# Masks through TensorE, three levels written in place, and two exponentials moved to the end of the in-projection, in a fused two-block kernel

## The chip, the cores and the metric

One core of a Trainium2 chip runs the whole program. The metric is device time in microseconds (us); the kernel before takes 3434.22 us, the median of three runs. Engine names are those of the profile: PE is TensorE (PEld its weight loads), DVE is VectorE, ACT is ScalarE, POOL is GpSimd, SP is SyncE, whose queue issues the loads of weights.

## What is computed

Two transformer-like blocks on 256 tokens of width 1024 run one after the other, each of two layers. The change lies in the first block, in the mixers of its two layers. Cut to what matters there:

```python
mod = cond @ w_ada[l] + b_ada[l]          # modulation, needed by later layers and sublayers
qa, fa, ia, ga, qb, kb, vb, ... = split((x * (1 + sc1) + sh1) @ w_in[l])
# mixer A, 4 heads of 128: a gated linear recurrence, as scores with decay
log_f = log(lb + (1 - lb) * sigmoid(fa));  k = (1 - lb) * sigmoid(-fa);  b = cumsum(log_f)
o_t = sum_{s <= t} (q_t . (k_s * exp(b_t - b_s))) v_s
oa = head_rms_norm(o) * silu(ga)
# mixer B, 8 heads of 64: stick-breaking attention, s < t only
z = q k^T / 8
w_ts = exp(log_sigmoid(z_ts) + sum_{s<j<t} log_sigmoid(-z_tj));   ob = w v
```

All values are float32.

## The kernel before

The 256 tokens are two tiles (TT) of 128. Each layer first runs `input_projection` (L1102): seven products of hT with 512 columns of `w_in`. A product's weights come in four quarters; ScalarE copies each quarter in rounded form (`split_hi`, L337) when TensorE has used up the quarter that held the place, and VectorE makes the remainder (L350). While the seventh product runs, ScalarE makes the rounded quarters of the tile that follows. VectorE takes the logarithms of the gates through `tensor_tensor_scan` (L1181), eight running sums over 128 tokens each, into B; that is done at the fifth product. The program is cut into blocks by hand (`nc.Block`), and every block begins and ends with a barrier of all five engines: the block of the in-projection ends at L3925, the mixer block begins at L1318.

The mixer block (`mixers`, L1302) runs both mixers at once, and its order is written out by hand for each engine.

*The recurrence.* For pairs of tokens s < t within 128, exp(b_t - b_s) is made in seven levels of halves, of 64, 32, 16, 8, 4, 2 and 1 tokens: with b at the end of a first half as the middle, exp(b_t - mid) goes to the queries of the second half and exp(mid - b_s) to the keys of the first. For each level n, VectorE subtracts (L1435, L1437), ScalarE takes one exponential over 128x1024 (L1401), VectorE multiplies into `qe` and `ke` (L1449, L1450), TensorE forms eight 128x128 products (4 heads by 2 tiles, L1353) in one of two PSUM units, and VectorE merges the right elements into `scores` with `copy_predicated` and a mask of that level (`take`, L1422). The diagonal (s = t) comes first (L1345). After the levels the cross-tile part, queries of tile 1 against keys of tile 0, takes the same way: L1458 and L1459, L1401, L1465 and L1466, L1363. At the end TensorE multiplies `scores` by the values (L1373, L1376), and VectorE copies the outputs (L1475). Each level's product also waits until `ke` and `qe` may be overwritten.

*Stick-breaking.* Four groups g of two heads (`StickBreaking`) are laid between the levels, one for two levels. `scores` (PE, L1229) forms the three causal 128x128 blocks of each head; `sizes` (ACT, L1259, L1260) copies them to Y and takes the absolute value L; `logs` (ACT, L1264, L1265) makes log(1 + exp(-L)), which needs another activation table than the exponential; `losses` (DVE, L1275) adds max(Y, 0) and then multiplies the two diagonal blocks by the 0/1 mask `before` (L1278); `sums` (PE, L1237 to L1239) forms suffix sums; `rest` (DVE, L1283) subtracts them and adds -1e30 on the masked elements of the diagonal blocks (L1285); `weights` (ACT, L1269) takes the exponential, `values` (PE, L1250, L1252) multiplies, `keep` (DVE, L1290, L1291) stores.

*The fills.* Between these steps TensorE forms the products of the modulation vectors of later sublayers (`beside`, L901): 24 halves of a tile in layer 0 and 20 in layer 1, 1 MB of weights each, how many where is written in `BESIDE_VALUES` and `BESIDE_LEVELS`. Four halves fit in the buffer `raw`: SP issues the load of a half when the fourth half before it has been used.

The orders of TensorE and ScalarE in that block are these loops (`n` counts levels, g = n // 2):

```python
for n in range(NL):                 # TensorE; odd n: stick.sums(g)
    stick_step(n)                   # even n: stick.scores(g), stick.values(g - 1), fill
    pe.wait_ge(vec_ready.sem, vec_ready.at(1 + n))
    ...                             # the level's products
    fill(BESIDE_LEVELS[l][n])
for n in range(NL + 1):             # ScalarE
    if n and n % 2 == 0:
        stick.sizes(act, s_, n // 2)
    act.wait_ge(cols_ready.sem, cols_ready.at(1 + n))
    act.activation(E[:], E[:], ACT.Exp).then_inc(act_ready.sem, 1)
    ...                             # n = 0: sizes(0); even n: logs, odd n: weights
```

## Time and profile before

| | before |
|---|---|
| median of 3 runs (lowest, highest) | 3434.22 us (3434.17, 3435.14) |
| span of the profiled execution, first to last instruction | 3432.0 us |
| TensorE / VectorE / ScalarE / GpSimd busy | 85% / 69% / 31% / 28% |
| mean granted clock of TensorE | 0.930 of full speed |
| mixer block, layer 0: first product to VectorE's copy of the outputs | 65.75 us |
| mixer block, layer 1: first instruction of VectorE to its copy of the outputs | 60.17 us |

The record of the profiled execution gives its span; the time of a run is taken around the program and is 2.2 us above that span at the median. A busy TensorE is not TensorE at its peak, and its two granted levels of clock in this trace are 0.50 (1.2 GHz) and 1.00 (2.4 GHz); a stretch in which it changes shows a value between. In the trace a float32 matmul appears as two rows, so eight products are "x16". In a timeline row the bracket says how long the engine was idle before the instruction and what released it.

### The profile page before, as it was taken

The page shows a single profiled execution, that of the slowest core. Times are in us where ns is not written, and L with a number is a line of the kernel's source. Part 1 is how long each engine was busy: PE and PEld are TensorE (multiplying, and loading weights), DVE is VectorE, ACT ScalarE, POOL GpSimd, SP SyncE. Part 2 cuts the span into 40 slices and gives each one's busy share as a digit, 9 for nine tenths or more (in the row PEclk, how much of TensorE's full clock was granted, in tenths as well). Part 3 has the DMA queues.
Part 4 walks back from the last instruction along what each step waited for, and adds up shares of the span by engine and source line. Part 5 has one row for each costly group of instructions (what it writes and reads, how often), then busy time and mean ns, then how long its engine had stood idle before and what let it go on. Part 6 is the DMA issues. An engine that isn't in the chain of part 4 may idle for free. (4 is left out here: it accounts for less than half of the span.)

```text
span 3432.0 us, 39790 instructions
## 1 busy us (share of the span) xinstructions
PE 2914.4 (85%) x14720; PEld 2169.4 (63%) x14720; DVE 2371.9 (69%) x3824; ACT 1048.4 (31%) x1586; POOL 971.8 (28%) x1028
## 2 busy tenths in 40 slices
PE   8899679948599879898699525777999999999999
PEld 6687368437387328685386212222788888887887
DVE  4657966677877766758876886565665765757665
ACT  3544110011100114543200101111444554546653
POOL 0000054555644670000354667777100000000000
PEclk9999689969799999998699758999999999999999
DMA  8765999999999996657999999999555455553253
GB/s 319 265 215 199 422 392 422 415 409 417 382 404 413 402 405 218 255 181 290 406 405 415 418 401 406 420 401 398 190 187 168 160 189 178 181 174 126 87 192 127
DMA packets 224262, 1034.12 MB, mean 301 GB/s; under 512 B 28784, under 2 KB 31344, under 8 KB 166256
## 3 DMA queue, kind: packets, MB, share of 16 engines
q0 software_dynamic: 147456, 536.94, 39.0%
q1 hardware_dynamic: 76656, 495.19, 39.0%
q8 instruction: 93, 1.52, 0.2%
q14 instruction: 57, 0.47, 0.0%
HBM read 1030.98 MB, written 1.05 MB: 301 GB/s over the span
## 5 line engine op out<-in xcount | busy, mean ns | idle before, releaser
L350 DVE TENSOR_TENSOR w_lo<-raw,w_hi 128x1024 fp32r<-128x1024 f32 (+1 forms) x460 | 546.9, 1204 | 415.1 <-ACT w_hi L337 414.0
L2238 POOL DMA_INDIRECT arena_layer<-in_peer_u,arena_layer x512 | 483.3, 944 | 1169.1 <-DVE arena_layer L2148 716.0
L2304 DVE CUSTOM_DVE_ANT_0 arena_layer<-arena_layer,ps 128x1024 f32<-128x1024 f32 x512 | 605.1, 1218 | 154.5 <-DMA arena_layer<-in_peer_u,arena_layer 124.9
L337 ACT ACTIVATE w_hi<-raw 128x1024 fp32r<-128x1024 f32 (+1 forms) x460 | 478.1, 1043 | 577.2 <-PE ps L745 371.1
L2300 DVE SCALAR_TENSOR_TENSOR ps<-arena_layer,ps 128x1024 f32<-128x1024 f32 x336 | 432.9, 1289 | 237.6 <-DMA arena_layer<-in_peer_v,arena_layer 225.7
L2238 POOL DMA_INDIRECT arena_layer<-in_peer_v,arena_layer x512 | 488.3, 954 | 272.7 <-DVE ps L2300 157.0
L801 PE MATMUL ps<-hT,w_hi 128*128 128x512 f32 x1376 | 479.7, 394 | 1.5 <-DVE hT L2956 1.5
L2338 PE MATMUL ps<-arena_layer,parts_context 128*128 128x512 f32 x704 | 351.1, 626 | 111.5 <-DMA arena_layer<-in_peer_v,arena_layer 104.5
L804 PE MATMUL ps<-hT,w_lo 128*128 128x256 f32 x1376 | 384.5, 279 | 0.0
L2338 PEld LDWEIGHTS ps<-arena_layer,parts_context 128*128 128x128 f32 x704 | 124.1, 194 | 335.7 <-issue 292.1
L745 PE MATMUL ps<-parts_context,w_whole 128*128 128x256 f32 x1216 | 271.3, 386 | 44.7 <-PEq L1044 44.7
L745 PE MATMUL ps<-hT,w_hi 128*128 128x256 f32 x1664 | 301.1, 284 | 4.1 <-DVE hT L1772 1.8
L801 PEld LDWEIGHTS ps<-hT,w_hi 128*128 128x128 f32 x1376 | 257.8, 187 | 61.6 <-issue 2.6
L745 PE MATMUL ps<-parts_context,raw 128*128 128x256 f32 x1280 | 280.6, 381 | 12.0 <-PEq L1044 12.0
L745 PEld LDWEIGHTS ps<-parts_context,w_whole 128*128 128x128 f32 x1216 | 235.6, 194 | 79.1 <-issue 45.9
L745 PEld LDWEIGHTS ps<-parts_context,raw 128*128 128x128 f32 x1280 | 244.8, 191 | 46.2 <-issue 12.4
L745 PEld LDWEIGHTS ps<-hT,w_hi 128*128 128x128 f32 x1664 | 259.4, 192 | 6.1 <-issue 6.0
L804 PEld LDWEIGHTS ps<-hT,w_lo 128*128 128x128 f32 x1376 | 259.6, 189 | 0.0
L745 PE MATMUL ps<-hT,w_lo 128*128 128x256 f32 x832 | 235.4, 283 | 0.0
L745 PE MATMUL ps<-w_hi,parts_ffn_x 128*128 128x512 f32 x704 | 220.7, 395 | 0.0
L745 PE MATMUL ps<-w_hi,hT 128*128 128x512 f32 x512 | 161.4, 397 | 4.1 <-DVE hT L1011 3.3
L745 PEld LDWEIGHTS ps<-hT,w_lo 128*128 128x128 f32 x832 | 159.6, 192 | 0.0
(405 smaller groups left out, 3500.2 us busy)
## 6 DMA issues: line engine op xcount, KB each, us to landing
raw<-in_ffn_w_gu SPq DMA_DIRECT2D x122, 1024.0 KB
raw<-in_ffn_w_down SPq DMA_DIRECT2D x54, 1024.0 KB
raw<-in_w_ada SPq DMA_DIRECT2D x44, 1024.0 KB
raw<-in_w_in SPq DMA_DIRECT2D x44, 1024.0 KB
raw<-in_w_mod SPq DMA_DIRECT2D x40, 1024.0 KB
w_whole<-in_w_mod SPq DMA_DIRECT2D x32, 1024.0 KB
w_whole<-in_ffn_w_gu SPq DMA_DIRECT2D x32, 1024.0 KB
raw<-in_conv_w_in SPq DMA_DIRECT2D x18, 1024.0 KB
```

The costliest lines, as they stand in the source:

```text
L337: act.activation(self.hi[:, k, 0:g.chunks(t)[k] * g.cols], self.part(g, t, slot, k // 2, g.starts(t, k), g.starts(t, k + 1)), ACT.Copy).th ...
L350: dve.tensor_tensor(self.lo[:, k, 0:n], self.part(g, t, slot, k // 2, g.starts(t, k), g.starts(t, k + 1)), self.hi[:, k, 0:n].bitcast(F32) ...
L745: mm = pe.matmul(out_, stay, move, start=start and n == 0, stop=stop and n == len(combos) - 1, skip_group_check=True)
L801: pe.matmul(both.rearrange("p (k t) -> p k t", k=2), high[:, c, cols], hT_both[:, :, row, :], start=row == 0, stop=False, skip_group_check ...
L804: mm = pe.matmul(both[:, 0:SEQ], low[:, c, cols], hT_hi[:, row, :], start=False, stop=row == last, skip_group_check=True)
L2238: gp.indirect_dma_start(self.grow[:, slot % GR, :], None, self.tables[slot // half_way], bass.IndirectOffsetOnAxis(ap=self.index[:, k:k + ...
L2300: dve.scalar_tensor_tensor(out=self.tile, in0=row, scalar=cell, in1=self.tile, op0=ALU.mult, op1=ALU.add) \
L2304: dve.tensor_tensor_reduce(row, row, self.tile, 1.0, 0.0, ALU.mult, ALU.add, cell).then_inc(row_used.sem, 1)
L2338: mm = pe.matmul(ps[:, t, cols], self.diagonals[:, side, r, :], self.grow[:, k % GR, cols], start=opens and r == 0, stop=True, skip_group_ ...
```

## The change

It does three things in the mixers of both layers.

1. *Masks of stick-breaking.* `scores` accumulates four more products, identity by `before_neg` (-1e30 on the masked elements, 0 elsewhere), onto the diagonal blocks of the scores in PSUM. The masking instructions of `losses` and `rest` on VectorE go, and with them the constant `before` and its load.
2. *Levels in place.* For the first three levels (DIRECT = 3: 64, 32, 16) TensorE forms only the small products that count, m by m, and writes each to its place in one PSUM unit: 8, 16 and 32 products instead of 8 each. One `take` with a merged mask reads all three, at the level of 8.
3. *Edge exponentials.* The exponentials of the first level and of the cross-tile part leave the mixer block. ScalarE makes them at the end of `input_projection`, from B directly: the subtraction becomes a bias operand, one instruction for each of 8 blocks and half (16 of 128x64), one of 128x4x128 and four of 128x128, into two new buffers in `side`. VectorE's subtractions for these two go, as does ScalarE's 128x1024 exponential for each.

In the rows below, `side_layer` holds the new buffers (first_E, cross_E), `rows` holds B, E and `qe`, `arena_layer` `ke` and `scores`, `w_hi` the rounded quarters, `columns` the identity.

ScalarE, end of layer 0's in-projection and start of the mixer block, before:

```order
L337 ACTIVATE w_hi<-raw 128x1024 [waits quarters_used,half_landed_3]
L337 ACTIVATE w_hi<-raw 128x1024 [waits quarters_used]
L3925 UNCONDITIONAL_BRANCH
L1393 UNCONDITIONAL_BRANCH [waits barrier_Pool_Activation_PE_DVE_SP_release]
L1401 ACT_TABLE_LOAD
L1401 ACTIVATE rows<-rows 128x1024 [waits cols_ready]
L1259 ACTIVATE arena_layer<-ps 128x768 [waits stick_scores_made]
L1260 ACTIVATE y_tok<-ps 128x768
```

and with the change:

```order
L338 ACTIVATE w_hi<-raw 128x1024 [waits quarters_used,half_landed_3]
L338 ACTIVATE w_hi<-raw 128x1024 [waits quarters_used]
L1215 ACTIVATE stat<-rows 128x8 [waits log_gates_summed]
L1218 ACT_TABLE_LOAD
L1218 ACTIVATE side_layer<-rows 128x64 x8
L1221 ACTIVATE side_layer<-rows,stat 128x64 [waits middle_sums_negated]
L1221 ACTIVATE side_layer<-rows,stat 128x64 x7
L1223 ACTIVATE side_layer<-rows 128x4x128
L1225 ACTIVATE side_layer<-rows 128x128 x4
L3970 UNCONDITIONAL_BRANCH
L1436 UNCONDITIONAL_BRANCH [waits barrier_Pool_Activation_PE_DVE_SP_release]
L1288 ACTIVATE arena_layer<-ps 128x768 [waits stick_scores_made]
```

The two branch rows are the end of one block and the start of the next, with the barrier between them. The new instructions stand after the last rounded quarter and before the barrier; the first 128x1024 exponential after the barrier is gone.

TensorE, layer 0's mixer block from the first scores to the second, before:

```order
L1229 MATMUL ps<-arena_layer 128x256 x2
L1229 MATMUL ps<-arena_layer 128x128 x2
L901 MATMUL ps<-first_layer_275,side_layer 32x512 [waits first_beside_tile_landed]
L901 MATMUL ps<-first_layer_275,side_layer 32x512 x7
L1353 MATMUL ps<-rows,arena_layer 128x128 [waits vec_ready]
L1353 MATMUL ps<-rows,arena_layer 128x128 x7
L901 MATMUL ps<-raw,side_layer 32x512 [waits half_landed_0]
```

and with the change:

```order
L1254 MATMUL ps<-arena_layer 128x128 x2
L1258 MATMUL ps<-before_neg,columns 128x128 x4
L904 MATMUL ps<-first_layer_274,side_layer 32x512 [waits first_beside_tile_landed]
L904 MATMUL ps<-first_layer_274,side_layer 32x512 x7
L1384 MATMUL ps<-rows,arena_layer 64x64 [waits vec_ready]
L1384 MATMUL ps<-rows,arena_layer 64x64 x7
L904 MATMUL ps<-raw,side_layer 32x512 [waits half_landed_0]
```

The four mask products stand between the scores and the first fill; the level of 64 has 64x64 products.

VectorE, layer 0, from the first `losses` to the first `keep`, before:

```order
L1275 SCALAR_TENSOR_TENSOR y_tok<-arena_layer,y_tok 128x768 [waits stick_logs_made]
L1278 TENSOR_TENSOR y_tok<-y_tok,before 128x2x2x128 [waits vec_step]
L1422 COPY_PREDICATED arena_layer<-level_mask,ps 128x1024 [waits pe_done]
L1449 TENSOR_TENSOR rows<-arena_layer,rows 128x16x32 [waits pe_done,act_ready,vec_step]
L1450 TENSOR_TENSOR arena_layer<-arena_layer,rows 128x16x32 [waits vec_step]
L1283 TENSOR_TENSOR y_tok<-arena_layer,ps 128x768 [waits stick_losses_summed,vec_ready]
L1285 TENSOR_TENSOR y_tok<-y_tok,before_neg 128x2x2x128 [waits vec_step]
L1435 TENSOR_TENSOR rows<-rows 128x32x16
L1437 TENSOR_TENSOR rows<-rows 128x32x16 [waits vec_step]
L1422 COPY_PREDICATED arena_layer<-level_mask,ps 128x1024 [waits pe_done]
L1290 CAST parts_layer<-ps 128x256 [waits stick_values_summed,vec_step]
L1291 TENSOR_TENSOR parts_layer<-ps,parts_layer 128x256 [waits vec_step]
```

and with the change:

```order
L1304 SCALAR_TENSOR_TENSOR y_tok<-arena_layer,y_tok 128x768 [waits stick_logs_made]
L1466 COPY_PREDICATED arena_layer<-level_mask,ps 128x1024 [waits pe_done]
L1496 TENSOR_TENSOR rows<-arena_layer,rows 128x16x32 [waits pe_done,act_ready,vec_step]
L1497 TENSOR_TENSOR arena_layer<-arena_layer,rows 128x16x32 [waits vec_step]
L1309 TENSOR_TENSOR y_tok<-arena_layer,ps 128x768 [waits stick_losses_summed,vec_ready]
L1480 TENSOR_TENSOR rows<-rows 128x32x16
L1482 TENSOR_TENSOR rows<-rows 128x32x16 [waits vec_step]
L1314 CAST parts_layer<-ps 128x256 [waits stick_values_summed]
L1315 TENSOR_TENSOR parts_layer<-ps,parts_layer 128x256 [waits vec_step]
```

Two masking instructions and one predicated copy are gone from this piece; the waits are the same.

The diff, cut to its core:

```diff
 LEVELS = (64, 32, 16, 8, 4, 2, 1)
+DIRECT = 3
...
+            edge_exponentials(act, B, *edges)
...
-                            dve.tensor_tensor_scan(
+                            ins = dve.tensor_tensor_scan(
                                 B[:, b * P:(b + 1) * P], ones[:], sg[:, h, m * P:(m + 1) * P], 0.0,
                                 ALU.mult, ALU.add)
+                    ins.then_inc(gates_summed.sem, 1)
...
+    def edge_exponentials(act, B, E, Ec):
+
+
+        m = LEVELS[0]
+        blocks = HG_HEADS * TT
+        b3, e3 = [ap.rearrange("p (b t) -> p b t", t=P) for ap in (B, E)]
+        b4, c4 = [ap.rearrange("p (h t m) -> p h t m", t=TT, m=P) for ap in (B, Ec)]
+        turned_middles = stat[:, 24:24 + blocks]
+        act.wait_ge(gates_summed.sem, gates_summed.at(1))
+        act.activation(turned_middles, b3[:, :, m - 1], ACT.Copy, scale=-1.0) \
+           .then_inc(middles_turned.sem, 1)
+        for b in range(blocks):
+            act.activation(e3[:, b, 0:m], b3[:, b, 0:m], ACT.Exp, bias=b3[:, b, m - 1:m], scale=-1.0)
+        act.wait_ge(middles_turned.sem, middles_turned.at(1))
+        for b in range(blocks):
+            ins = act.activation(e3[:, b, m:P], b3[:, b, m:P], ACT.Exp, bias=turned_middles[:, b:b + 1])
+        ins.then_inc(edge_expd.sem, 1)
+        act.activation(c4[:, :, 1, :], b4[:, :, 1, :], ACT.Exp)
+        for h in range(HG_HEADS):
+            ins = act.activation(c4[:, h, 0, :], b4[:, h, 0, :], ACT.Exp,
+                                 bias=b4[:, h, 0, P - 1:P], scale=-1.0)
+        ins.then_inc(edge_expd.sem, 1)
...
-                    mm = pe.matmul(self.bank[n][:, cols], self.kb[at, g, keys], self.qb[at, g, queries],
-                                   start=True, stop=True)
+                    pe.matmul(self.bank[n][:, cols], self.kb[at, g, keys], self.qb[at, g, queries],
+                              start=cols.start == 0, stop=False, skip_group_check=True)
+            for n in range(2):
+                for cols in (slice(0, P), slice(SEQ, self.WIDTH)):
+                    mm = pe.matmul(self.bank[n][:, cols], ident[:], before_neg[:],
+                                   start=False, stop=True, skip_group_check=True)
             mm.then_inc(sb_scored.sem, 1)
...
-            v.link(dve.scalar_tensor_tensor(out=L, in0=self.Y, scalar=0.0, in1=L,
-                                            op0=ALU.max, op1=ALU.add))
-            mask = before[:].unsqueeze(1).unsqueeze(1).to_broadcast([P, 2, 2, P])
-            dve.tensor_tensor(self.edges(L), self.edges(L), mask, ALU.mult).then_inc(sb_lost.sem, 1)
+            dve.scalar_tensor_tensor(out=L, in0=self.Y, scalar=0.0, in1=L,
+                                     op0=ALU.max, op1=ALU.add).then_inc(sb_lost.sem, 1)
 
         def rest(self, dve, v, g):
-            S = self.S
             dve.wait_ge(sb_summed.sem, sb_summed.at(g + 1))
-            v.link(dve.tensor_tensor(S, self.Y, self.banks, ALU.subtract))
-            neg = before_neg[:].unsqueeze(1).unsqueeze(1).to_broadcast([P, 2, 2, P])
-            dve.tensor_tensor(self.edges(S), self.edges(S), neg, ALU.add).then_inc(sb_left.sem, 1)
+            dve.tensor_tensor(self.S, self.Y, self.banks, ALU.subtract).then_inc(sb_left.sem, 1)
...
+                def level_in_place(m):
+
+
+                    for b in range(blocks):
+                        for first in range(0, P, 2 * m):
+                            keys = slice(b * P + first, b * P + first + m)
+                            queries = slice(b * P + first + m, b * P + first + 2 * m)
+                            mm = pe.matmul(ps[first:first + m, 0, queries], ke[:, keys], qe[:, queries],
+                                           start=True, stop=True, skip_group_check=True)
+                    return mm
...
                     pe.wait_ge(vec_ready.sem, vec_ready.at(1 + n))
-                    for b in range(blocks):
-                        mm = pe.matmul(ps[:, (n + 1) % 2, b * P:(b + 1) * P],
-                                       ke[:, b * P:(b + 1) * P], qe[:, b * P:(b + 1) * P],
-                                       start=True, stop=True)
+                    if n < DIRECT:
+                        mm = level_in_place(LEVELS[n])
+                    else:
+                        for b in range(blocks):
+                            mm = pe.matmul(ps[:, unit_of(n + 1), b * P:(b + 1) * P],
+                                           ke[:, b * P:(b + 1) * P], qe[:, b * P:(b + 1) * P],
+                                           start=True, stop=True)
...
-                    if n and n % 2 == 0:
+                    if n % 2 == 0:
                         stick.sizes(act, s_, n // 2)
-                    act.wait_ge(cols_ready.sem, cols_ready.at(1 + n))
-                    act.activation(E[:], E[:], ACT.Exp).then_inc(act_ready.sem, 1)
-                    if n == 0:
-                        stick.sizes(act, s_, 0)
+                    if 0 < n < NL:
+                        act.wait_ge(cols_ready.sem, cols_ready.at(n))
+                        act.activation(E[:], E[:], ACT.Exp).then_inc(act_ready.sem, 1)
...
                 def take(n):
 
+                    if 1 <= n < DIRECT:
+                        return
                     dve.wait_ge(pe_done.sem, pe_done.at(n + 1))
-                    mask = level_mask[:, n, :].unsqueeze(1).to_broadcast([P, blocks, P])
+                    mask = level_mask[:, n and n + 1 - DIRECT, :].unsqueeze(1).to_broadcast([P, blocks, P])
                     v.link(dve.copy_predicated(
                         scores.rearrange("p (b t) -> p b t", t=P), mask,
-                        ps[:, n % 2, :].rearrange("p (b t) -> p b t", t=P)))
+                        ps[:, unit_of(n), :].rearrange("p (b t) -> p b t", t=P)))
...
+                    e_lo, e_hi = halves(E if n else first_E)
+                    if n:
+                        b_lo, b_hi = halves(B)
+                        mid = b_lo[:, :, m - 1:m].to_broadcast([P, nb, m])
+                        v.tick(dve.tensor_tensor(e_hi, b_hi, mid, ALU.subtract))
+                        v.wait()
+                        dve.tensor_tensor(e_lo, mid, b_lo, ALU.subtract).then_inc(cols_ready.sem, 1)
...
-                    dve.wait_ge(act_ready.sem, act_ready.at(1 + n))
                     if n >= 1:
+                        dve.wait_ge(act_ready.sem, act_ready.at(n))
                         dve.wait_ge(pe_done.sem, pe_done.at(n + 1))
+                    else:
+                        dve.wait_ge(edge_expd.sem, edge_expd.at(1))
                     v.link(dve.tensor_tensor(halves(qe)[1], halves(q_all)[1], e_hi, ALU.mult))
...
-                v.link(dve.tensor_copy(te[:, :, 1, :], tb[:, :, 1, :]))
-                dve.tensor_tensor(te[:, :, 0, :], tb[:, :, 0, P - 1:P].to_broadcast([P, HG_HEADS, P]),
-                                  tb[:, :, 0, :], ALU.subtract).then_inc(cols_ready.sem, 1)
+                tiles = [ap.rearrange("p (h t m) -> p h t m", t=TT, m=P) for ap in (cross_E, qe, ke, q_all, k_all)]
+                te, tq, tk, tqa, tka = tiles
                 stick.losses(dve, v, NL // 2)
                 take(NL - 1)
-                dve.wait_ge(act_ready.sem, act_ready.at(1 + NL))
+                dve.wait_ge(edge_expd.sem, edge_expd.at(2))
```

## Rows read from the trace of the kernel before

**Rows 1.** Page, part 1: busy time, share of the span and instructions of each engine.

```profile
PE 2914.4 (85%) x14720; PEld 2169.4 (63%) x14720; DVE 2371.9 (69%) x3824; ACT 1048.4 (31%) x1586; POOL 971.8 (28%) x1028
```

**Rows 2.** Stretches, the two mixer blocks: length, each engine's busy time, PEclk, DMA share, GB/s.

```profile
120.39:186.14 65.75, 59.35 (x458) 36.07 (x460) 47.75 (x64) 36.76 (x38) 0.00 (x0) 0.96 0.90 358
...
1380.87:1441.04 60.17, 54.60 (x426) 35.14 (x428) 47.71 (x63) 36.74 (x38) 0.00 (x0) 0.97 0.86 327
```

**Rows 3.** Timeline of VectorE, layer 1: start, length, engine, line, operation, [idle before <-releaser].

```profile
1379.25 1.22 DVE L1193 COPY arena_layer<-ps 128x1024 f32<-128x1024 f32 x1
...
1380.87 0.69 DVE L1435 TENSOR_TENSOR rows<-rows 128x512 f32<-128x512 f32 x1 [0.40 <-PEq L3925]
...
1389.90 0.96 DVE L1275 SCALAR_TENSOR_TENSOR y_tok<-arena_layer,y_tok 128x768 f32<-128x768 f32 x1 [3.63 <-ACT y_tok L1265]
...
1390.90 0.69 DVE L1278 TENSOR_TENSOR y_tok<-y_tok,before 128x512 f32<-128x512 f32 x1
...
1391.51 1.30 DVE L1422 COPY_PREDICATED arena_layer<-level_mask,ps 128x1024 f32<-128x1024 uint32 x1
...
1392.85 0.69 DVE L1449 TENSOR_TENSOR rows<-arena_layer,rows 128x512 f32<-128x512 f32 x1
...
1400.75 0.69 DVE L1449 TENSOR_TENSOR rows<-arena_layer,rows 128x512 f32<-128x512 f32 x1 [0.72 <-ACT rows L1401]
...
1406.59 0.69 DVE L1449 TENSOR_TENSOR rows<-arena_layer,rows 128x512 f32<-128x512 f32 x1
...
1427.23 0.72 DVE L1449 TENSOR_TENSOR rows<-arena_layer,rows 128x512 f32<-128x512 f32 x1 [0.30 <-ACT rows L1401]
...
1441.04 1.23 DVE L1475 COPY y_tok<-ps 128x1024 f32<-128x1024 f32 x1 [3.04 <-PE ps L1376]
```

**Rows 4.** Timeline of ScalarE, layer 1.

```profile
1377.02 1.06 ACT L337 ACTIVATE w_hi<-raw 128x1024 fp32r<-128x1024 f32 x1 [1.60 <-PE ps L745]
...
1403.63 1.28 ACT L1401 ACT_TABLE_LOAD   x1
...
1404.92 1.06 ACT L1401 ACTIVATE rows<-rows 128x1024 f32<-128x1024 f32 x1
```

**Rows 5.** Timeline of TensorE, layer 0's mixer block.

```profile
120.39 3.75 PE L1345 MATMUL ps<-arena_layer 128*128 128x128 f32 x16 [3.88 <-PEq L3925]
...
162.33 1.06 PE L901 MATMUL ps<-raw,side_layer 128*32 128x512 f32 x8 [0.92 <-DMA raw<-in_w_ada]
...
177.20 1.06 PE L901 MATMUL ps<-raw,side_layer 128*32 128x512 f32 x8 [0.91 <-DMA raw<-in_w_ada]
```

**Rows 6.** Timeline of ScalarE elsewhere: small instructions.

```profile
828.78 7.12 ACT L3391 ACTIVATE rows<-columns 128x128 f32<-128x128 f32 x24 [30.26 <-PEq L3335]
...
190.11 0.21 ACT L1409 ACTIVATE stat<-stat 128x8 f32<-128x8 f32 x1 [5.92 <-DVE stat L1480]
...
190.23 0.57 ACT L1941 COPY side_layer<-ps 128x512 f32<-128x512 f32 x1
```

**Rows 7.** Timeline of TensorE, layer 1.

```profile
1380.86 2.84 PE L1345 MATMUL ps<-arena_layer 128*128 128x128 f32 x16 [3.88 <-PEq L3925]
...
1394.32 2.05 PE L1353 MATMUL ps<-rows,arena_layer 128*128 128x128 f32 x16 [0.65 <-DVE arena_layer L1450]
...
1438.06 1.38 PE L1373 MATMUL ps<-arena_layer 128*128 128x128 f32 x10 [0.51 <-DVE arena_layer L1471]
...
1448.20 1.04 PE L1386 MATMUL ps<-columns,y_tok 128*128 128x128 f32 x8
...
1448.99 0.48 PE L745 MATMUL ps<-hT,w_hi 128*128 128x256 f32 x2
```

**Rows 8.** Stretches of 1 us at the two blocks' starts, columns as before.

```profile
120.00:121.00 1.00, 0.61 (x3) 0.65 (x4) 0.61 (x1) 0.66 (x1) 0.00 (x0) 0.50 0.00 0
...
1381.00:1382.00 1.00, 1.00 (x10) 1.00 (x10) 0.97 (x2) 1.00 (x1) 0.00 (x0) 0.94 0.37 66
```

**Rows 9.** Timeline of TensorE elsewhere: a train of narrow products.

```profile
325.61 3.84 PE L1843 MATMUL ps<-arena_layer 64*128 64x128 f32 x64 [1.10 <-ACT arena_layer L1858]
```

More of the change, by code:

```diff
@@ L3946, in _build @@
             assert beside.tiles == BESIDE_MIXERS[l]
-            input_projection(block, l, qa, sg, km, ia, ga, qb, kb, vb, rows[:, 0, :], (rows[:, 2, :], ke, scores),
-                             beside, arrive)
+            edges = [side[:, 1024 + k * D:1024 + (k + 1) * D] for k in range(2)]
+            input_projection(block, l, qa, sg, km, ia, ga, qb, kb, vb, rows[:, 0, :], edges,
+                             (rows[:, 2, :], ke, scores), beside, arrive)
         oaT, obT = (oa_hi, oa_lo), (ob_hi, ob_lo)
```

48 lines of the change are left out of this document (22 added, 26 removed).

## The prediction

> **What bounds the kernel now.** I read four views in this order: the page for the engines' shares, the timelines of VectorE, ScalarE and TensorE over the two mixer blocks, the table of stretches for TensorE's granted clock, and single rows elsewhere for prices. Over the whole span TensorE is busy 85% and VectorE 69% [rows 1], but the change touches two blocks of 65.75 and 60.17 us, one in each layer [rows 2], so only their own rows count.
>
> In layer 1, the mixer block begins when VectorE has evacuated the last product of the in-projection: that copy ends at 1379.25 + 1.22 = 1380.47 and VectorE's first instruction starts at 1380.87 [rows 3]. ScalarE has finished its last split copy at 1377.02 + 1.06 = 1378.08 [rows 4] and waits for the block's barrier. Inside the block, which I take up to VectorE's copy of the outputs at 1441.04, VectorE looks like the bound after TensorE, whose list is padded with fills: it is busy 47.7 of 60.2 us [rows 2]. But its two longest idle stretches, 3.63 us before the first `losses` and 3.04 us before the output copy [rows 3], are waits for the others. Between them runs a ring: products of a level on TensorE, a fill, the scores of the next head pair, ScalarE's `sizes`, its exponential, and the next pair of products on VectorE. From the level-32 products (1392.85) to the level-16 ones (1400.75) this ring takes 7.90 us, and from those to the level-8 ones (1406.59) it is 5.84 us [rows 3], of which ScalarE (log, table load, exponential ending at 1404.92 + 1.06 [rows 4]) sets 5.26. So VectorE and the ring are within a microsecond of each other: work taken off VectorE alone soon turns into waiting.
>
> In layer 0 a third thing bounds: the weights of the side modulation. TensorE waits for them at 162.33 and 177.20 [rows 5]; six 1 MB halves lie between, 2.48 us each.
>
> **The change, part by part.** All sums are made against the profiled execution, whose span is 3432.0 us; the median of the runs is 3434.2, and the 2.2 us around the span I leave as they are.
>
> *ScalarE's new tail.* The edge exponentials stand behind all four split copies, and the last of these waits for TensorE's last quarter. Nothing hides them there: the barrier takes them. Per layer: one 8-column copy 0.21; a table load, 1.29 until the next instruction starts (1403.63 to 1404.92 [rows 4]); sixteen 64-column exponentials with a bias operand; one of 512 columns, 0.57; four of 128 columns. A train of twenty-four 128-column instructions with an operand of that kind takes 7.12 us, 0.30 each; an 8-column one lasts 0.21, and the next one starts 0.12 after it [rows 6]. I take 0.25 for 64 columns, between 0.21 and 0.30; the ends are 0.12 and 0.30. Sum: 0.21 + 1.29 + 16 x 0.25 + 0.57 + 4 x 0.30 = 7.27, so ScalarE ends at 1385.35, 4.9 us after VectorE's copy. The block starts **4.9 us later** (2.8 to 5.7), in both layers: **+9.8** (5.6 to 11.4).
>
> The table load shows as 1.28, and the exponential behind it starts at once [rows 4]. The Trainium skill (ScalarE: Activation LUTs, What ACT_TABLE_LOAD costs) adds a drain of about 1.38 us to every switch of sets; by that rule the tails would cost 2.8 us more and the sum would end at 3450. The row decides: the time from load to exponential holds no such drain.
>
> *What VectorE sheds per layer.* The first level's two subtractions and the cross pair, four masks of 0.69 in `losses` (1390.90), as many in `rest` and two predicated copies of 1.30 (1391.51) [rows 3]: some 11 us. What arrives at the end is decided by the ring, place by place, in layer 1:
>
> (a) Block start to the level-32 products. The path is TensorE's diagonal and scores, then ScalarE. The sixteen diagonal rows took 2.84 in layer 1 [rows 7] and 3.75 in layer 0 [rows 5], where the granted clock was 0.50 from the start, while layer 1's began at 0.94 [rows 8]. TensorE now idles 4.9 us longer before them, so I price both at 3.75: +0.9. The four mask products are eight rows of 128x128: 0.79 from such a train's start to the next product at full clock (1448.20 to 1448.99 [rows 7]), 8 x 3.75/16 = 1.9 at half. I take 0.9 for this group. Behind `losses`, VectorE's shed mask leaves ScalarE's exponential as the last wait: 0.6 earlier. Together +1.2. Taking the first level's subtractions off saves nothing here, since VectorE waits for `losses` anyway.
>
> (b) Level 32 to level 16. The mask stands between the scores and `sizes`, on the ring: +0.8. The level's products were 16 rows in 2.05 us (1394.32 [rows 7]) and are now 32 rows of 32x32. No such small product is in the trace. The quickest train is that of the expert keys, 64 rows of 128 columns in 3.84 us with its last row's drain, 0.057 each [rows 9]; scaled to 32 columns it is 0.014. Between 0.014 and 0.057 I take 0.045, nearer to the row that exists: 1.4 us, -0.5. Sum +0.3.
>
> (c) Level 16 to 8: ScalarE's 5.26 in place of VectorE's 5.84, **-0.6**. Level 16 is now 64 rows, 2.9 us, and just hides.
>
> (d) Level 8 to 4. TensorE must do those 2.9 us, a fill and the sums before the level-8 products, and is 0.7 late for them; with the mask **+1.5**.
>
> (e) Level 4 to 2: as (c), -0.6. (f) Level 2 to 1: the mask again, +0.8. (g) From there to the output copy (13.81 before, 1427.23 to 1441.04 [rows 3]): the output product at 1438.06 [rows 7] waits for VectorE's list, which sheds two masks: -1.3. The cross pair sat ahead of a wait for ScalarE's logs, so it gives nothing.
>
> Layer 1's block: 1.2 + 0.3 - 0.6 + 1.5 - 0.6 + 0.8 - 1.3 = **+1.3**. With small products at 0.014, (b) falls by 1.0 and (d) by 0.7, to -0.4; at 0.057 plus a cold mask, +3.
>
> By the Trainium skill (TensorEngine Tiling (Array Packing), Instruction Overhead) a small matmul costs some 60 cycles however few its columns, an estimate of 0.025 at full clock; the sum would then end near 3445. No row here shows a product that small.
>
> Layer 0's block: the diagonal ran at half clock already, so (a) is +0.3. A half is loaded when the fourth before it has been used, so each lateness of TensorE's fills is handed to the loads, and a gain is not: at 2.48 us each there is nothing to catch up with. Two fills instead of one stand behind level 16. I take **+2.0**, between one mask (+0.8) and three masks with the late level-8 products (+3.2).
>
> *Edits at nothing.* The late load of the constant `before` disappears from a queue that is waited for only much later. The exponentials that leave the mixers (1.06 us each [rows 4]) lay beside other waits.
>
> Sum: 9.8 + 1.3 + 2.0 = 13.1, on the span 3432.0 + 13.1 = 3445.1; with the 2.2 around it 3447.3 us.
>
> **The rivals.**
>
> *VectorE is the bound after all (not slower).* If the mask products ran ahead of the wait for ScalarE at no cost, layer 1's block would shorten by all that VectorE sheds, 11 us; layer 0, on its loads, would gain nothing. 9.8 - 11 = -1.2: 3433. It decides where the ring is under VectorE's list by over 1 us per head pair. For it: VectorE's 47.7 busy of 60.2 us [rows 2]. Against: the ring's 7.90, with the mask inside it.
>
> *The tail is hidden.* If ScalarE could make the exponentials in the gaps between its split copies, the barrier would not move, and 1.3 + 2.0 is left: 3437.5, within the bound of 0.2% (6.9 us, about what can be told from no change). The written order speaks against it.
>
> *Both new trains are cheap.* Tails at 2.8 each, small products at 0.014: 5.6 - 0.4 + 0.8 = 6.0, so 3440.2.
>
> *Small products are dear.* If each costs what a 128x128 row does, 0.11, level 32 takes 3.5 and level 16 takes 7.0: the level-8 products wait 3.3 longer and level 32 adds 2.1, some 5.5 us in each layer: 3458. For it: products with 128 stationary columns pace at the same 0.10 [rows 7]. Against: the train at 0.057 [rows 9].
>
> **How the numbers follow.** Forecast 0.72, dear 0.09, cheap 0.08, hidden tail 0.05, VectorE-bound 0.06. Faster by over 0.2% takes half of the last: 0.03. Within 0.2% are the other half, the hidden tail and half of cheap: 0.12. Slower: 0.85. The range runs from 3440 (cheap) to 3454 (upper ends of the tail and of both blocks, 11.4 + 3 + 3.2 = 17.6, and 2 towards dear): it leaves out the dear case, the VectorE-bound one and the hidden tail, 0.2 together.
>
> **What would show it.** In the changed profile: ScalarE's train of 64-column exponentials after the last split copy and before the barrier, ending 4 to 5.5 us behind VectorE's copy; TensorE idle over 8 us there; VectorE waiting for ScalarE's exponentials at the even levels, longer than before; mask products of about 0.8 us between scores and `sizes`; the time from first VectorE instruction to output copy no shorter than 60.2 in layer 1 and, from TensorE's first product, 65.75 in layer 0. I am wrong if the barrier moves by under 2 us, or if a block shortens by more than 2.

## The result and the profile after

Five runs of the changed kernel have a median of 3447.15 us (3441.56 to 3451.45); five of the kernel before, beside them, 3434.47 us (3434.17 to 3435.19). The ratio is 1.0033, with a 95% interval of 1.0023 to 1.0044: the change costs 8 to 15 us, 12.7 by the medians. The forecast was 3447.3. The profiled execution of the changed kernel took 3447.29 us; its span is 3445.5 us, 13.5 above the one before. One run of the kernel before beside the first four experiments took 7576.38 us, a slow one, and is left out of the ranges and counts below (it moves the median of its group by 0.07).

Part 1 of the page after answers to [rows 1]. VectorE lost 20.8 us of work over the whole program (2371.9 to 2351.1), ScalarE gained 6.7, and TensorE has 192 rows more and is not busier:

```profile
PE 2912.5 (85%) x14912; PEld 2170.2 (63%) x14912; DVE 2351.1 (68%) x3796; ACT 1055.1 (31%) x1626; POOL 969.7 (28%) x1028
```

The stretches of the changed kernel, in the columns of [rows 2]. The first and third rows are new: from the end of VectorE's last copy of the in-projection to the start of the block. The second and fourth answer to the two blocks.

```profile
120.39:125.38 4.99, 0.00 (x0) 0.03 (x1) 0.00 (x0) 4.63 (x18) 0.00 (x0) 0.50 0.00 0
125.38:196.87 71.49, 61.75 (x554) 38.25 (x556) 37.35 (x50) 33.38 (x35) 0.00 (x0) 0.92 0.88 336
1390.55:1395.55 5.00, 0.00 (x1) 0.04 (x1) 0.00 (x0) 4.63 (x18) 0.00 (x0) 0.50 0.00 0
1395.55:1456.08 60.53, 55.42 (x522) 36.12 (x524) 37.29 (x50) 33.38 (x35) 0.00 (x0) 0.97 0.85 318
```

The barrier used to open 0.40 us after that copy in layer 1 [rows 3] and 0.39 after it in layer 0 (the rows of VectorE before, below); now it opens 4.99 and 5.00 after, so it moved by 4.6 us in each layer. The blocks themselves went from 65.75 to 71.49 (+5.74) and from 60.17 to 60.53 (+0.36), although VectorE does 10.4 us less in each. With 0.39 that layer 0's in-projection ended later, this makes 0.39 + 4.60 + 5.74 + 4.60 + 0.36 = 15.7; the program outside the blocks was 2.2 us shorter in this execution, which leaves the 13.5.

```profile
118.78 1.22 DVE L1193 COPY arena_layer<-ps 128x1024 f32<-128x1024 f32 x1
120.39 0.69 DVE L1435 TENSOR_TENSOR rows<-rows 128x512 f32<-128x512 f32 x1 [0.39 <-PEq L3925]
```

ScalarE's timeline at layer 1's barrier shows the tail as forecast, all of it behind the last split copy:

```profile
1387.10 1.06 ACT L338 ACTIVATE w_hi<-raw 128x1024 fp32r<-128x1024 f32 x1 [1.60 <-PE ps L748]
1388.06 0.20 ACT L1215 ACTIVATE stat<-rows 128x8 f32<-128x8 f32 x1
1388.27 1.28 ACT L1218 ACT_TABLE_LOAD   x1
1389.57 2.02 ACT L1218 ACTIVATE side_layer<-rows 128x64 f32<-128x64 f32 x8
1391.49 2.00 ACT L1221 ACTIVATE side_layer<-rows,stat 128x64 f32<-128x64 f32 x8
1393.40 0.61 ACT L1223 ACTIVATE side_layer<-rows 128x512 f32<-128x512 f32 x1
1393.92 1.26 ACT L1225 ACTIVATE side_layer<-rows 128x128 f32<-128x128 f32 x4
```

It ends at 1395.18, 4.63 us after VectorE's copy. In VectorE's timeline of the same block, the waits of [rows 3] have grown or come anew: 7.60 us before the first losses (3.63 before), 2.10 before the first head pair's values are kept (0.63 before), 1.41 before the level-8 products. The rows of L1496 are the starts of the levels 64, 32, 16, 8, 4, 2 and 1:

```profile
1389.33 1.22 DVE L1197 COPY arena_layer<-ps 128x1024 f32<-128x1024 f32 x1
1395.55 0.69 DVE L1496 TENSOR_TENSOR rows<-arena_layer,side_layer 128x512 f32<-128x512 f32 x1 [5.01 <-PEq L3970]
...
1406.02 0.96 DVE L1304 SCALAR_TENSOR_TENSOR y_tok<-arena_layer,y_tok 128x768 f32<-128x768 f32 x1 [7.60 <-ACT y_tok L1294]
...
1408.45 0.69 DVE L1496 TENSOR_TENSOR rows<-arena_layer,rows 128x512 f32<-128x512 f32 x1 [0.24 <-DVE arena_layer L1466]
...
1414.29 0.42 DVE L1314 CAST parts_layer<-ps 128x256 fp32r<-128x256 f32 x1 [2.10 <-PE ps L1281]
...
1415.95 0.69 DVE L1496 TENSOR_TENSOR rows<-arena_layer,rows 128x512 f32<-128x512 f32 x1 [0.78 <-ACT rows L1445]
...
1421.21 0.69 DVE L1496 TENSOR_TENSOR rows<-arena_layer,rows 128x512 f32<-128x512 f32 x1 [1.41 <-ACT rows L1445]
...
1430.20 0.69 DVE L1496 TENSOR_TENSOR rows<-arena_layer,rows 128x512 f32<-128x512 f32 x1 [0.71 <-ACT rows L1445]
...
1435.51 0.69 DVE L1496 TENSOR_TENSOR rows<-arena_layer,rows 128x512 f32<-128x512 f32 x1 [0.23 <-DVE arena_layer L1466]
...
1443.50 0.72 DVE L1496 TENSOR_TENSOR rows<-arena_layer,rows 128x512 f32<-128x512 f32 x1 [0.70 <-ACT rows L1445]
...
1456.08 1.22 DVE L1519 COPY y_tok<-ps 128x1024 f32<-128x1024 f32 x1 [3.18 <-PE ps L1419]
```

TensorE's timeline there shows the new products. The masks (L1258) last 1.16, and the next product starts 1.09 behind their start. The 32 rows of 32x32 (16 products of two rows each) are over in half a microsecond (the next product at 1410.40), the 64 rows of 16x16 in 0.70:

```profile
1395.55 3.75 PE L1373 MATMUL ps<-arena_layer 128*128 128x128 f32 x16 [8.49 <-PEq L3970]
...
1400.25 1.16 PE L1258 MATMUL ps<-before_neg,columns 128*128 128x128 f32 x8
1401.34 1.93 PE L904 MATMUL ps<-first_layer,side_layer 128*32 128x512 f32 x16
...
1409.93 0.66 PE L1384 MATMUL ps<-rows,arena_layer 128*32 128x32 f32 x29 [0.87 <-DVE arena_layer L1497]
1410.40 0.62 PE L904 MATMUL ps<-raw,side_layer 128*32 128x512 f32 x1
...
1412.27 1.16 PE L1258 MATMUL ps<-before_neg,columns 128*128 128x128 f32 x8
1413.36 0.66 PE L1279 MATMUL ps<-y_tok,arena_layer 128*64 128x256 f32 x4
...
1417.43 0.70 PE L1384 MATMUL ps<-rows,arena_layer 128*16 128x16 f32 x64 [0.48 <-DVE arena_layer L1497]
```

In layer 0, TensorE's timeline holds the surprise: a wait of 3.33 us for a weight, and behind it sums that last nearly twice as long (1.22 where layer 1 has 0.70), since the granted clock was 0.50 from 186 to 190 us (the stretches below it):

```profile
167.22 1.06 PE L904 MATMUL ps<-raw,side_layer 128*32 128x512 f32 x8 [1.33 <-DMA raw<-in_w_ada]
...
185.36 1.94 PE L904 MATMUL ps<-raw,side_layer 128*32 128x512 f32 x8 [3.33 <-DMA raw<-in_w_ada]
187.23 1.22 PE L1266 MATMUL ps<-y_tok,tri 128*128 128x256 f32 x2
```

```profile
186.00:188.00 2.00, 2.00 (x10) 0.69 (x3) 0.00 (x0) 0.00 (x0) 0.00 (x0) 0.50 1.03 434
188.00:190.00 2.00, 2.00 (x9) 1.73 (x8) 0.00 (x0) 0.00 (x0) 0.00 (x0) 0.50 0.97 307
```

### The profile page after: what moved, and what is told of

Read it like the earlier page. It is cut to its first block and busy times, and to the rows that moved or that the text cites. A ratio compares the mean times of both kernels' runs of the same rounds, so it can differ in the third digit from the quotient of the medians.

```text
span 3445.5 us, 40185 instructions
## 1 busy us (share of the span) xinstructions
PE 2912.5 (85%) x14912; PEld 2170.2 (63%) x14912; DVE 2351.1 (68%) x3796; ACT 1055.1 (31%) x1626; POOL 969.7 (28%) x1028
```

## The experiments

The theory: the tail shifts both barriers and does nothing else; inside the blocks the masks on TensorE cost and the small products gain, both on the ring; what VectorE sheds is worth little. The rivals: VectorE's list bounds, small products are dear, the tail's shift is absorbed. In the rows after the table's first, medians are of 5 to 12 runs each, beside 26 to 30 of the kernel before on the same chip. Those of the kernel before scattered over 13 to 15 us in each of three series (3429.15 to 3443.79 in the first), so a total is known to 3 or 5 us only, and the traces decide: below, "block" is the time from the end of VectorE's last in-projection copy to the start of its copy of the outputs, 66.14 us in layer 0 and 60.57 in layer 1 in the kernel before, of which there is one profile. Of the two kernels that were profiled twice, layer 1's block came out alike to 0.1 and 0.3 us, layer 0's only to 4.6 and 2.6; so layer 1 carries the argument.

| kernel | median, us | before beside it | ratio, 95% interval | block, layer 0 | block, layer 1 |
|---|---|---|---|---|---|
| changed kernel, first profile | 3447.15 | 3434.47 | 1.0023 to 1.0044 | 76.48 | 65.53 |
| changed kernel, second profile | 3442.86 | 3430.79 | 1.0023 to 1.0044 | 71.90 | 65.59 |
| its exponentials spread out | 3438.83 | 3433.77 | 0.9995 to 1.0016 | 67.88 | 61.50 |
| its exponentials in the mixer | 3439.91 | 3433.77 | 1.0011 to 1.0031 | 65.15 | 60.74 |
| its masks on VectorE | 3440.89 | 3433.77 | 1.0006 to 1.0033 | 68.49 | 63.90 |
| in place for one level only | 3450.38 | 3433.77 | 1.0025 to 1.0054 | 73.43 | 67.77 |
| tail alone | 3440.70 | 3433.90 | 1.0013 to 1.0033 | 71.09 | 65.32 |
| small products alone | 3426.55 | 3430.79 | 0.9981 to 0.9999 | 64.48 | 58.49 |
| small products alone, again | 3430.97 | 3433.90 | 0.9984 to 1.0002 | 67.03 | 58.81 |
| small products, exponentials spread | 3430.99 | 3430.79 | 0.9983 to 1.0002 | 64.07 | 58.84 |
| the same, scores first | 3429.92 | 3430.79 | 0.9982 to 1.0003 | 64.71 | 58.84 |
| the same, fills moved | 3433.34 | 3433.90 | 0.9992 to 1.0015 | 67.85 | 60.24 |

**The exponentials between the split copies.** ScalarE's function becomes a generator that stops after the negated middles, one, seven and six more exponentials:

```diff
+            pieces = edge_exponentials(act, B, *edges)
             for t in range(n):
-                split_ahead(act=act, tile=(t, t % 2, t // 2))
+                for k in range(QUARTERS):
+                    split_ahead(act=act, tile=(t, t % 2, t // 2), quarters=(k,))
+                    if t == n - 1 or (t, k) == (5, 2):
+                        next(pieces, None)
...
-            edge_exponentials(act, B, *edges)
```

> The changed kernel with ScalarE's edge exponentials issued between the split copies of the in-projection's last tile instead of behind them: the negated middles after a copy of the tile before, one exponential after the first of the last four copies, seven after the second, six after the third, the rest (some 2.4 us) after the fourth. Theory (the tail is a plain shift of both barriers, 4.6 us each, and the blocks behind keep their lengths): both barriers come back to within 0.5 us of VectorE's copy, 9 us fewer, 3437 to 3440 us. Rival one (the loads of layer 0 absorb an earlier start): only layer 1's 4.6 comes back, 3442 to 3444. Rival two (the pieces delay the split copies, and VectorE's halves and copy behind them): the barrier moves back by under 2 us, 3443 or more.

The theory held. ScalarE's timeline in layer 0: the last split copy starts at 116.94 as in the changed kernel, with most of the train now in the gaps ahead of it, and the last exponential ends at 120.15, before VectorE's copy does (120.38). The barrier opens 0.39 behind that copy again, in both layers. The block of layer 1 is 4.0 us shorter than the changed kernel's, and the median lies 5.1 us above the kernel before, where the changed kernel's two lie 12.7 and 12.1 above.

```profile
110.38 1.28 ACT L1222 ACT_TABLE_LOAD   x1
111.68 0.35 ACT L1222 ACTIVATE side_layer<-rows 128x64 f32<-128x64 f32 x1
111.93 1.04 ACT L338 ACTIVATE w_hi<-raw 128x1024 fp32r<-128x1024 f32 x1
112.88 1.77 ACT L1222 ACTIVATE side_layer<-rows 128x64 f32<-128x64 f32 x7
...
118.89 1.26 ACT L1234 ACTIVATE side_layer<-rows 128x128 f32<-128x128 f32 x4
```

**The exponentials back in the mixer.** The first level's and the cross pair's subtractions and exponentials stand where the kernel before has them:

```diff
-                    if 0 < n < NL:
-                        act.wait_ge(cols_ready.sem, cols_ready.at(n))
-                        act.activation(E[:], E[:], ACT.Exp).then_inc(act_ready.sem, 1)
+                    act.wait_ge(cols_ready.sem, cols_ready.at(1 + n))
+                    act.activation(E[:], E[:], ACT.Exp).then_inc(act_ready.sem, 1)
...
-            edge_exponentials(act, B, *edges)
```

> The changed kernel with the first level's and the cross-tile exponentials (and VectorE's subtractions for them) back in the mixer; masks through TensorE and three levels by small products stay. Theory: no tail, so 9 us fewer; VectorE's four extra instructions lie beside its waits for the losses and for ScalarE's logs: 3437 to 3440 us, within 1.5 us of the kernel with the spread exponentials. Rival (what the edges take off VectorE is worth time in the block): 3441 to 3444, clearly above the kernel with the spread exponentials.

The median is in the theory's range, 1.1 us from the one with the spread exponentials. In layer 1 the block is even 0.76 us shorter than with them: making these exponentials early is worth nothing to the block.

**The masks back on VectorE.** `scores`, `losses` and `rest` as in the kernel before, with the constant `before` and its load:

```diff
-            for n in range(2):
-                for cols in (slice(0, P), slice(SEQ, self.WIDTH)):
-                    mm = pe.matmul(self.bank[n][:, cols], ident[:], before_neg[:],
-                                   start=False, stop=True, skip_group_check=True)
...
+            dve.tensor_tensor(self.edges(L), self.edges(L), mask, ALU.mult).then_inc(sb_lost.sem, 1)
...
+            dve.tensor_tensor(self.edges(S), self.edges(S), neg, ALU.add).then_inc(sb_left.sem, 1)
```

> The changed kernel with the causal mask back on VectorE (two masking instructions of 0.69 us per head pair), the four mask products per head pair gone from TensorE. Theory (the mask products lie on the ring between scores and sizes, 1.1 us each group, while VectorE has room): the level-32 to level-16 step, the level-8 to level-4 step and the level-2 to level-1 step shorten by about 1 us each, layer 0's block likewise or more, in all 3 to 6 us fewer: 3441 to 3444 us. Rival (VectorE's list is the bound, so 5.5 us more of it per layer costs): 3449 to 3455.

The stretches of the two blocks, from the first instruction:

```profile
125.19:188.68 63.49, 54.92 (x522) 32.09 (x524) 42.83 (x58) 33.40 (x35) 0.00 (x0) 0.97 0.93 370
1387.69:1446.59 58.90, 51.34 (x490) 32.25 (x492) 42.80 (x58) 33.39 (x35) 0.00 (x0) 0.96 0.89 339
```

VectorE has 5.5 us more to do in layer 1 than in the changed kernel, and the block is 1.63 us shorter (58.90 against 60.53). The steps say where: level 32 to 16 takes 6.64 instead of 7.50, 8 to 4 7.91 instead of 8.99, 2 to 1 6.91 instead of 7.99, while 4 to 2 gives 0.5 back and the end 1.3 (13.88 instead of 12.58). So for the masks VectorE's list bounds at those two places alone, 1.8 us together; each of these three masks on TensorE costs the ring 0.9 to 1.1 us. The median, 3440.89, lies just under the theory's range.

**In place for one level only.**

```diff
-DIRECT = 3
+DIRECT = 1
```

> The changed kernel with the in-place small products for the first level alone (16 rows of 64x64); levels 32 and 16 by whole 128x128 products with predicated copies of their own again. Theory (a small product costs 0.01 us and hides): VectorE gets two copies of 1.3 us more per layer, which lie in its waits: within 2 us of the changed kernel, 3445 to 3449. Rival one (small products are dear and hold TensorE up): 3 us or more below the changed kernel. Rival two (the predicated copies were worth their time): 3450 or more.

The theory's range was missed on the high side. The median lies in the second rival's range, but not for its reason: level 32 to 16 takes 8.98 instead of 7.50, and VectorE's extra copy there lies ahead of a wait of 2.44 us for TensorE:

```profile
1410.19 1.30 DVE L1466 COPY_PREDICATED arena_layer<-level_mask,ps 128x1024 f32<-128x1024 uint32 x1
1413.93 0.42 DVE L1314 CAST parts_layer<-ps 128x256 fp32r<-128x256 f32 x1 [2.44 <-PE ps L1281]
```

The whole products last 2.05 us there, and the fill, scores, mask and ScalarE's exponential queue behind them. So the small products gain 1.5 us at this place and 2.2 in layer 1's block, more than I had given them.

**The changed kernel once more,** unedited:

> The changed kernel once more, unedited, for a second profile and more times beside runs of the kernel before on this chip. Theory (the 3.33 us wait for a weight of the side modulation in layer 0, and the half clock behind it, were that one execution's; the change's own price there is the tail and the masks): from VectorE's last in-projection copy to the output copy 71 to 72.5 us in layer 0 and 65 to 66 in layer 1; median 3444 to 3448. Rival (the wait belongs to the change): again 75 us or more in layer 0 with a wait over 2.5 us, median 3447 to 3451.

The traces went as the theory has it; the median is 12.1 us above the kernel before, with both lower than on the first chip, so that the median itself lies under the theory's range. Layer 0's block was 4.6 us shorter than in the first profile, nearly all of it between the level-1 products and the output copy (15.17 instead of 19.38). TensorE's longest waits for weights were these, and the granted clock stayed at 1.00 behind both:

```profile
166.45 1.07 PE L904 MATMUL ps<-raw,side_layer 128*32 128x512 f32 x8 [2.00 <-DMA raw<-in_w_ada]
182.97 1.07 PE L904 MATMUL ps<-raw,side_layer 128*32 128x512 f32 x8 [1.70 <-DMA raw<-in_w_ada]
```

**The small products alone,** twice; the masks are back on VectorE and the exponentials back in the mixer, in one kernel:

> The in-place small products for levels 64, 32 and 16 alone: masks on VectorE and all exponentials in the mixer, as in the kernel before. Theory (the parts add: small products give 1.5 to 2.5 us per layer, masks on TensorE and the tail take): from copy to output copy 58.5 to 59.5 us in layer 1 (60.57 before) and 63.5 to 65.5 in layer 0 (66.14 before), median 3429 to 3432, 2 to 5 us below the kernel before. Rival (the small products gain only when VectorE's other work is gone): 60 us or more in layer 1, median within 1.5 us of the kernel before.

> The kernel with the small products alone once more, unedited, for a narrower interval. Theory (layer 0's block 1.7 and layer 1's 2.1 us shorter): again 58 to 59 us in layer 1 and 64 to 65 in layer 0, the median 2 to 5 us below the kernel before. Rival (the gain of its first runs was scatter): the median within 1.5 us of the kernel before.

The stretches of the two blocks in the first of the two, from the first instruction:

```profile
121.24:185.32 64.08, 55.76 (x522) 32.52 (x524) 45.32 (x62) 36.75 (x38) 0.00 (x0) 0.96 0.92 366
1381.80:1439.89 58.09, 50.84 (x490) 31.35 (x492) 45.27 (x61) 36.73 (x38) 0.00 (x0) 0.97 0.89 342
```

Layer 1's block was 2.1 and 1.8 us shorter than before. Layer 0's was 1.7 shorter in one execution and 0.9 longer in the other, so what it gains there is not settled. In the longer one TensorE waited 1.75 us for a weight and ran its sums at a lower clock behind it (0.61 over 145 to 149 us; in the other the wait was 1.31, with full clock behind it), and the step from level 8 to 4 took 10.41 us instead of 8.31:

```profile
144.61 1.06 PE L905 MATMUL ps<-raw,side_layer 128*32 128x512 f32 x8 [1.75 <-DMA raw<-in_w_ada]
145.60 0.99 PE L1266 MATMUL ps<-y_tok,tri 128*128 128x256 f32 x2
```

The medians lie 4.2 and 2.9 us below the kernel before; the first interval excludes 1, the second just does not. It is the fastest version that was run twice, below both kernels each time by its medians.

**The small products with the exponentials spread out.**

> Small products, and ScalarE's edge exponentials spread between the split copies; masks on VectorE. Theory (spread out, the edges cost nothing, and gain nothing in the block since VectorE waits for the losses anyway): layer 1 from copy to output copy 59 to 60 us, layer 0 64 to 65.5, median 3430 to 3433, within 1.5 us of the kernel with small products alone. Rival (the edges off VectorE are worth time once neither tail nor mask takes it): 58 us or less in layer 1, and a median 2 us or more below the kernel with small products alone.

Layer 1's block is 58.84, as with the small products alone (58.49 and 58.81), and the rival's 58 or less was not seen. The median, though, lies 4.4 us above that of the small products alone on the same chip, outside the theory's 1.5; the two blocks differ by -0.4 and +0.35 us, so they do not show where it comes from, and it is of the size of the scatter.

**The same with the scores first.** The sixteen diagonal products go behind the first head pair's scores:

```diff
                     if g:
                         stick.values(pe, g - 1)
+                    else:
+                        diagonal()
                     fill(BESIDE_VALUES[l][g])
```

> As the last one, with the first head pair's scores ahead of the sixteen diagonal products on TensorE. Theory (the block's start is a chain of diagonal, scores, sizes, logs and losses; with the scores first the diagonal's 3.75 us lie beside ScalarE, until TensorE's own list bounds, 10.4 us): the level-32 products come 1 to 2 us earlier than in the kernel with the scores second, in both layers; layer 1 58 to 59 us, median 3428 to 3431. Rival (TensorE's list already bounds the start): under 0.5 us.

The level-32 products did come early, by 3.1 us in layer 1 (9.33 after the copy instead of 12.40) and by 3.5 in layer 0. Yet the block is as long: in layer 1, TensorE's timeline shows a new wait for weights, behind which the fill and the sums come late and run at 0.50 of the clock (1401.9 to 1404.9), and the steps from level 32 to 4 take 3.1 us longer together:

```profile
1398.72 0.70 PE L1403 MATMUL ps<-rows,arena_layer 128*16 128x16 f32 x64 [0.47 <-DVE arena_layer L1516]
1401.92 1.93 PE L905 MATMUL ps<-raw,side_layer 128*32 128x512 f32 x8 [2.51 <-DMA raw<-in_w_ada]
```

The block's start is gained and the loads take it back. So I moved fills.

**The same with fills moved.** The first two halves go ahead of the diagonal, and layer 1's half behind level 16 goes behind level 2:

```diff
-BESIDE_LEVELS = ((2, 1, 2, 1, 2, 1, 2, 2), (2, 1, 1, 1, 1, 0, 1, 2))
+BESIDE_LEVELS = ((2, 1, 2, 1, 2, 1, 2, 2), (2, 1, 0, 1, 1, 1, 1, 2))
```

> As the kernel with the scores first, and two fills of the side modulation moved: the first two halves ahead of the diagonal products, and in layer 1 the half behind level 16 to behind level 2. Theory (with the scores first the blocks are bound by the loads of the side modulation's weights, which start when a half has been used): layer 0 from copy to output copy 61 to 63 us instead of 64.7, layer 1 56 to 57.5 instead of 58.8, the median 4 to 8 us below the kernel before on the same chip. Rival (the wait for the ring comes back at another place): layer 0 within 0.7 us of 64.7 and layer 1 of 58.8, the median within 2.5 us of the kernel before.

A miss. Layer 0 grew to 67.85 and layer 1 to 60.24. In layer 0 the two fills now ran right behind the idle stretch and took 3.64 us instead of 1.9, and a wait of 3.00 us for weights ended at 145.30, with sums of 1.12 us instead of 0.70 behind it. What would make use of the early start stays open.

**The tail alone.** Masks on VectorE and `DIRECT = 1` (the first level's products of 64x64 stay), with the tail left as it is in the changed kernel:

> ScalarE's tail alone: the edge exponentials behind the split copies as in the changed kernel, masks on VectorE, levels 32 and 16 by whole products with copies of their own; the first level alone by products of 64x64. Theory (the tail shifts both barriers by 4.6 us and the block keeps its length): from copy to output copy 70 to 72 us in layer 0 and 64.5 to 66 in layer 1, the median 8 to 10 us above the kernel before. Rival (VectorE's and ScalarE's lighter block gives part of it back): under 64 us in layer 1, the median 6 us or less above the kernel before.

The blocks came out at 71.09 and 65.32, 4.95 and 4.75 above the kernel before, as the theory had it; layer 1 does not give part of it back. The median, 6.8 us up, lies between theory and rival, within the scatter.

## Why the prediction was right, and where its terms were off

The sum was 13.1 us on the span: 9.8 for the tails, 1.3 for layer 1's block, 2.0 for layer 0's. The difference of medians is 12.7, and in the second profile the two blocks together are 10.8 longer. The mechanism of the main term is right; that the total came within half a microsecond is luck. In the profiled execution the tails and layer 1's block fell short of the forecast by 1.5 us, layer 0's block was 3.7 over it, and the rest of the program happened to take most of that back (+0.4 and -2.2); and a total is known to 3 or 5 us only.

*The tail* was forecast at 4.9 per layer and measured 4.6 in the changed kernel, 4.75 and 4.95 as the block's growth by itself. The sixteen 64-column exponentials take 4.02 us, 0.25 each, as taken. The row decided rightly about the rule in the Trainium skill (ScalarE: Activation LUTs, What ACT_TABLE_LOAD costs): its drain of 1.38 us does not show here either, as the copy ahead of the load ends at 1388.26, the load starts at 1388.27 and the exponential at 1389.57, 1.30 later.

*Layer 1's block,* by the steps of the prediction:

| step | forecast | measured |
|---|---|---|
| (a) start to the level-32 products (11.98 to 12.90) | +1.2 | +0.92 |
| (b) level 32 to 16 (7.90 to 7.50) | +0.3 | -0.40 |
| (c) level 16 to 8 (5.84 to 5.26) | -0.6 | -0.58 |
| (d) level 8 to 4 (7.90 to 8.99) | +1.5 | +1.09 |
| (e) level 4 to 2 (5.83 to 5.31) | -0.6 | -0.52 |
| (f) level 2 to 1 (6.91 to 7.99) | +0.8 | +1.08 |
| (g) level 1 to the output copy (13.81 to 12.58) | -1.3 | -1.23 |
| sum | +1.3 | +0.36 |

The rows of VectorE before from which (d) to (f) are taken, beside those of [rows 3], are the level-4 and the level-2 products:

```profile
1414.49 0.69 DVE L1449 TENSOR_TENSOR rows<-arena_layer,rows 128x512 f32<-128x512 f32 x1 [0.72 <-ACT rows L1401]
...
1420.32 0.69 DVE L1449 TENSOR_TENSOR rows<-arena_layer,rows 128x512 f32<-128x512 f32 x1
```

Two terms were mis-sized, in opposite directions. The mask products were priced at 0.8 from a train at full clock [rows 7] and cost 1.09 from their start to the next product, also at full clock, hence (f). The small products were priced at 0.045 a row, near the narrowest train there was [rows 9]; they take 0.47 us to the next product for 32 rows, 0.015 each, and 0.70 for 64 rows with the last one's drain, 0.011 each. So the lateness of 0.7 in (d) did not come, and (b) turned into a gain. The rule in the Trainium skill (TensorEngine Tiling (Array Packing), Instruction Overhead), some 60 cycles for each matmul, an estimate of 0.025, is too dear if every row counts as a matmul, which the prediction leaves open; counted by product, of two rows each, the trace shows 0.029 and 0.022 and agrees with it. Its total of 3445 is 2 us from the forecast, less than the scatter, so the medians do not decide between the two.

The term (c) belongs to the small products: with them alone the step is 5.26 too, as the one merged copy leaves VectorE a copy less there. One sign did not come as written: at levels 16, 4 and 1 VectorE waits 0.70 to 0.78 us for ScalarE's exponential, where it waited 0.30 to 0.72; what grew is the wait ahead of it, for the values of the head pair.

*Layer 0's block* was forecast at +2.0. The profiled execution showed +5.74, the second one 71.90 - 66.14 - 4.60 = +1.16. The first holds the 3.33 us wait and the half clock behind it, which the second does not; the mechanism (loads of the side modulation) was the one named, but how long TensorE waits for them differs from execution to execution by more than the term. Why it does is not shown, and neither is the change's own part in layer 0.

*The rivals.* VectorE as the bound fell: with 10.4 us less work on it layer 1's block got no shorter, and with 5.5 us of masks given back it got 1.6 shorter. Dear small products fell with the 0.011. Cheap products were half of the third rival, and true; the tail at 2.8 was not. The hidden tail did not happen as written, but the kernel that spreads the exponentials out fits its price: 5.1 us above the kernel before by the medians (interval -1.7 to 5.5) against a forecast of 3.3.

*By parts,* in layer 1's block: the tail +4.75 (alone), the masks +1.6 to +2.3 (changed kernel against masks on VectorE; mixer exponentials against small products alone, 60.74 against 58.49 and 58.81), the small products -1.4 to -2.2 (with the tail alone, the kernel before, and the tail with masks as the base). The parts add up to the 5.0 measured: along one order, 4.75 - 1.42 + 1.63.

## What to carry to other kernels

Work that is taken off a busy engine is worth only what the chain through it loses: here VectorE shed 10.4 us per layer, and layer 1's block gave back 2.3 of it ((c), (e) and (g)), while the masks, put on the chain through TensorE and ScalarE, cost 3.45 at four places against the 1.8 that they freed. Work moved "into the tail" of a stage sits on the barrier unless each piece is written ahead of the instruction whose wait makes the gap; the same 7 us in those gaps left the barrier where it was. And an edit of several parts should be tried part by part: one of the three gained here, and the other two took more than it gave.

## What the hardware showed that was not expected

Products with 16 or 32 columns and as many stationary ones follow each other at 0.011 and 0.015 us a row (two rows to a product), four to five times quicker than the train of 128 columns (0.057 [rows 9]), all at a granted clock of 1.00.

TensorE's clock after a wait differs between executions. After the 8.5 us of idling that the tail makes, the sixteen diagonal rows took 3.61 to 3.75 us in every kernel and layer; after 3.9 us they took from 2.02 to 3.75. Inside a block, the length of the wait does not tell what follows. Waits of 1.70 and 2.00 us (the changed kernel's second profile) were followed by full clock; one of 1.75 (the small products alone, again) was followed by 0.61 over 145 to 149 us, one of 2.51 (scores first) by 0.50 over 1401.9 to 1404.9 us, one of 3.00 (fills moved) by 0.57 over 146 to 150 us, and one of 3.33 (the changed kernel's first profile) by 0.50 over 186 to 190 us. The two executions of the changed kernel whose layer 0 differ by 4.6 us differ in that, and so do the two of the small products alone.
